# The selection of keys for tokens 128 to 255 moves behind the convolution, and tokens 0 to 127 get no index scores

## The reference, cut to what matters

```
topk = min(TOPK_MAX, seq // 4)                     # 128
limit = (q_pos // CHUNK + 1) * CHUNK               # CHUNK 64
visible = key_pos[None, :] < limit[:, None]
rel = relu(einsum('bqhd,bsd->bqhs', iqb, ik))      # 4 index heads of 64
score = einsum('bqhs,bqh->bqs', rel, iwb)
score = where(visible[None], score, -inf)
_, idx = lax.top_k(score, topk)
valid = idx < limit[None, :, None]
```

## Time and profile before

| | us |
|---|---|
| median of 3 runs | 3282.81 |
| lowest, highest | 3281.57, 3286.73 |
| profiled execution, its own time | 3312.99 |
| its span | 3311.1 |

### The profile page before, as it was taken

How to read it: one execution, slowest core, us unless ns; L and a number is a source line. 1 busy time by engine, 2 the same in 40 slices (tenths; PEclk the granted TensorE clock), 3 DMA queues, 4 the chain that set the end, 5 groups by cost and what they waited for, 6 DMA issues and landing times. The chain is left out here.

```text
span 3311.1 us, 41588 instructions
## 1 busy us (share of the span) xinstructions
PE 2814.8 (85%) x14662; PEld 2084.6 (63%) x14662; DVE 1630.6 (49%) x3068; ACT 993.3 (30%) x1557; POOL 749.0 (23%) x353
## 2 busy tenths in 40 slices
PE   3996777986987787986986889999997988789997
PEld 2784355334775264324884678878886856678886
DVE  6786643335786743236715664643638143441113
ACT  4524422114524422114215631111113231231222
POOL 1430021111430021110320032222323300134443
PEclk9987887998987887997998989999998986699999
DMA  6630017953620027952611021322423210022222
GB/s 235 227 116 33 1 54 303 345 205 123 241 97 31 1 92 295 350 199 80 220 66 58 14 77 58 134 102 77 159 72 113 95 54 1 26 101 92 99 92 73
DMA packets 92342, 398.13 MB, mean 120 GB/s; under 512 B 16384, under 2 KB 18080, under 8 KB 70816
## 3 DMA queue, kind: packets, MB, share of 16 engines
q1 hardware_dynamic: 63248, 303.36, 25.7%
q0 software_dynamic: 28800, 92.30, 7.5%
q10 hardware_dynamic: 144, 0.52, 0.0%
HBM read 489.98 MB, written 23.59 MB: 155 GB/s over the span
## 5 line engine op out<-in xcount | busy, mean ns | idle before, releaser
L2414 DVE TENSOR_TENSOR ffn_silu<-ffn_silu,PS 128x512 f32<-128x512 f32 x66 | 37.6, 597 | 414.6 <-ACT ffn_silu L2396 414.6
L391 POOL TENSOR_TENSOR 19_w_part<-weights_raw,19_w_part 128x2048 fp32r<-128x2048 f32 (+2 forms) x44 | 146.3, 3327 | 406.5 <-ACT 19_w_part L347 406.5
L2147 PE MATMUL PS<-one_weights_more,11_h_tokens 128*64 128x512 f32 (+1 forms) x1024 | 230.9, 603 | 2.6 <-ACT 11_h_tokens L2199 1.7
L233 PE MATMUL PS<-ffn_h_parts,19_w_part 128*128 128x512 f32 (+1 forms) x640 | 203.5, 338 | 8.6 <-DVE ffn_out_t L1687 7.8
L234 PE MATMUL PS<-ffn_h_parts,19_w_part 128*128 128x512 f32 (+1 forms) x640 | 202.4, 338 | 0.0
L391 POOL TENSOR_TENSOR 33_w_part<-weights_raw,33_w_part 128x2048 fp32r<-128x2048 f32 (+2 forms) x36 | 149.4, 4150 | 212.6 <-ACT 33_w_part L347 212.6
L391 POOL TENSOR_TENSOR 3_w_part<-weights_raw,3_w_part 128x1024 fp32r<-128x1024 f32 (+1 forms) x52 | 142.3, 2737 | 237.5 <-ACT 3_w_part L347 237.4
L2147 PEld LDWEIGHTS PS<-one_weights_more,11_h_tokens 128*64 128x64 f32 x1024 | 78.4, 139 | 132.8 <-issue 129.0
L233 PE MATMUL PS<-one_mix_h_parts,3_w_part 128*128 128x512 f32 x352 | 144.3, 410 | 20.2 <-ACT 3_w_part L347 20.2
L2396 ACT ACTIVATE ffn_silu<-PS 128x512 f32<-128x512 f32 x66 | 32.4, 526 | 404.0 <-PE PS L238 378.4
L234 PE MATMUL PS<-one_mix_h_parts,3_w_part 128*128 128x512 f32 x352 | 142.3, 404 | 0.0
(11 more groups left out here) (630 smaller groups left out, 6994.9 us busy)
## 6 DMA issues: line engine op xcount, KB each, us to landing
one_weights_more<-in_w_gu SPq DMA_DIRECT2D x128, 1024.0 KB, 8.7
one_weights_more<-in_w_down SPq DMA_DIRECT2D x64, 1024.0 KB, 8.4
weights_raw<-in_f_gu SPq DMA_DIRECT2D x44, 1024.0 KB, 4.8
one_values<-in_w_ada POOLq DMA_DIRECT2D x32, 1024.0 KB, 6.7
weights_raw<-in_w_proj SPq DMA_DIRECT2D x60, 512.0 KB, 3.4
ffn_shared<-in_w_ada POOLq DMA_DIRECT2D x24, 1024.0 KB, 7.1
weights_raw<-in_w_ada SPq DMA_DIRECT2D x32, 512.0 KB, 9.0
two_ab_mod_w<-in_w_ada POOLq DMA_DIRECT2D x16, 1024.0 KB, 5.4
```

The lines of the kernel that those rows point to most:

```text
L233: nc.tensor.matmul(out, w[0], x[1], start=(j == 0), stop=False)
L391: self.nc.gpsimd.tensor_tensor(self.part[:, u, 1], self.raw[:, u], self.part[:, u, 0].bitcast(F32), ALU.subtract).then_inc(self.count["spl ...
L2147: mm = nc.tensor.matmul(M.PS[rows(h), 2 + i % 2, :], h_[:, i % 2, k, rows(h)], weights(i, h, k * 2 * FE), start=(k == 0), stop=(k == KD - 1))
L2414: ins = nc.vector.tensor_tensor(sl[:, u, off:off + nt], sl[:, u, off:off + nt], M.PS[:, 4 * u + 2 + a, 0:nt], ALU.mult)
```

## The change

- `Values` keeps item 1 only (384 keys, tile 2), so its TensorE queue is: scores 1, chunk 0, chunk 1, chunk 2, chunk 3. Behind the selection VectorE writes tile 0's bias with the two memsets (`choose_all`, with a semaphore of its own).
- Item 3 (the 128-key scores of tile 0) is not computed any more, neither its matmuls nor VectorE's reads and sums.
- Item 2 (256 keys, tile 1) goes to `convolve`. TensorE issues its four matmuls behind the turned row of line 766, VectorE does the selection behind its last convolution. It has one bank, number 7, and a scratch of its own; three semaphores are added.

```diff
--- before.py
+++ after.py
@@ -662,7 +662,7 @@
 def convolve(nc, M, A, l, B):
 
 
-    s = take(M, "par step conv gates sig act_step ab_done tr cp dec_in")
+    s = take(M, "par step conv gates sig act_step ab_done tr cp dec_in scored taken chosen")
     rows = NH_M
     with ExitStack() as ctx:
         cw = ctx.enter_context(M.nc.sbuf_tensor(f"{M.blocks}_conv_w", [P, 4, CONV + 1], F32))
@@ -676,6 +676,9 @@
         a = ctx.enter_context(M.nc.sbuf_tensor(f"{M.blocks}_i_rel", [rows, T], F32))
         am = ctx.enter_context(M.nc.sbuf_tensor(f"{M.blocks}_i_max", [rows, T], F32))
         th = ctx.enter_context(M.nc.sbuf_tensor(f"{M.blocks}_floor", [rows, T], F32))
+
+        keys = SelectKeys(nc, M, {"scored": s["scored"], "taken": s["taken"], "step": s["chosen"]}, B, range(2, 3), (7,),
+                          SelectKeys.scratch(nc, M, ctx))
         block = ctx.enter_context(nc.Block())
 
         @block.sync
@@ -724,6 +727,7 @@
             nc.vector.tensor_scalar(th[:], th[:], -1.0, 80.0, ALU.mult, ALU.min).then_inc(s["ab_done"], 1)
             for c in range(1, 4):
                 conv(c)
+            keys.choose(dve)
 
         @block.scalar
         def _(act):
@@ -766,6 +770,7 @@
                 mm = nc.tensor.transpose(M.PS[:, 6, t * NH_M:(t + 1) * NH_M], a[:, t * P:(t + 1) * P],
                                          M.K[0:rows, K_ID:K_ID + rows])
             mm.then_inc(s["tr"], 1)
+            keys.scores(pe, 2)
     give(nc, s)
 
 
@@ -821,10 +826,6 @@
                     dve.wait_ge(s["taken"], n + 1)
                     step(nc.vector.tensor_tensor(sc[:, 0:w], sc[:, 0:w], tmp[:, 0:w], ALU.add))
 
-            if t == 0:
-                step(nc.vector.memset(B.bias[:, 0, 0:w], 0.0))
-                step(nc.vector.memset(B.bias[0:64, 0, 64:w], NEG))
-                continue
             step(nc.vector.memset(sc[0:64, w - 64:w], -3.0e38))
             src = sc
             for r in range(TOPK // 8):
@@ -833,6 +834,12 @@
                 src = work
             step(nc.vector.tensor_tensor(tmp[:, 0:w], work[:, 0:w], sc[:, 0:w], ALU.is_equal))
             step(nc.vector.tensor_scalar(B.bias[:, t, 0:w], tmp[:, 0:w], NEG, None, ALU.mult))
+
+    def choose_all(self, dve):
+
+        step = Steps(dve, self.s["all"])
+        step(self.nc.vector.memset(self.B.bias[:, 0, 0:P], 0.0))
+        step(self.nc.vector.memset(self.B.bias[0:64, 0, 64:P], NEG))
 
 
 def attend(nc, M, items, scale):
@@ -2616,9 +2623,9 @@
 
     def __init__(self, nc, M, ctx, weights, N, out, tiles, following, before, B=None, scratch=None):
         self.nc, self.M, self.N, self.out, self.tiles, self.before = nc, M, N, out, tiles, before
-        self.s = s = take(M, STREAM + "psum_free copied scored taken step")
+        self.s = s = take(M, STREAM + "psum_free copied scored taken step all")
         self.S = Stream(nc, M, ctx, s, weights, N, following, before.S)
-        self.K = SelectKeys(nc, M, s, B, range(1, TT), (2, 3, 6, 7), scratch) if B else None
+        self.K = SelectKeys(nc, M, s, B, range(1, 2), (2, 3, 6, 7), scratch) if B else None
 
     def free(self, eng, n):
         eng.wait_ge(self.s["psum_free"], n + 3)
@@ -2671,13 +2678,14 @@
         elif self.before.H:
             pe.wait_ge(self.before.s["h_done"], len(self.before.H.order))
         for n in range(N):
-            if K and n + 1 < TT:
+            if K and n + 1 in K.which:
                 K.scores(pe, n + 1)
             S.one(pe, chunk, n, n % 2)
 
     def vector(self, dve):
         if self.K:
             self.K.choose(dve)
+            self.K.choose_all(dve)
 
     def scalar(self, act):
         nc, M, s, S = self.nc, self.M, self.s, self.S
```

## The result

| | median | runs, lowest to highest |
|---|---|---|
| before | 3286.73 us | 5, 3281.57 to 3301.82 |
| changed | 3318.29 us | 5, 3310.22 to 3326.03 |

A forecast was written before the change was run, and what follows sets the result against it. TensorE was taken to bound the projection's block and ScalarE the convolution's end, where VectorE had 6.49 us of slack. -30.8 + 40.5 + 1.0 = +10.7 us on 3282.81 gave 3293.5 us, range 3285 to 3301.

The forecast's parts named there:

- The projection's block: Value projection: TensorE's wait, the scores and the slow restart go; 16.0 us less in layer 0, 14.8 in layer 1.
- take 11.3: Third value chunk's length in us without the wait, bounded by the fourth's 10.88 and the second's 11.62.
- rival 4: Projection's block: another wait holds the third or fourth chunk, a tenth to a third of 30.8 us unsaved; chance 0.05.
- Behind the convolution: End of the convolution block: the moved 256-key scores and selection add 20.2 us per layer, 40.5 together.
- the cycle: Behind the convolution: one head's score matmul, VectorE's read and handovers over the one bank, 1.81 us.
- Rival 2: Behind the convolution: TensorE at 2.4 GHz, only +15.2 us per layer, not slower, 3282.4 us; chance 0.08.
- The rule of the Trainium skill: Convolution's small matmuls: sustained activity releases the throttle, so 10.9 us of back-to-back matmuls should have gone to 2.4 GHz.
- A cost of +1.0: Attention: starting after an 18 us TensorE idle costs 1.0 us in all, ends 0 and +3.
- rival 3: Attention longer at the low clock after the idle, or handovers 0.4 us dearer: +14 to +18 us; chance 0.09.
- The median of the runs shown: Whole kernel before: base time of 3282.81 us to which the +10.7 us was added.
- (its three runs lie over 5.2 us): Whole kernel: ground for taking 0.2%, 6.6 us, as about what a measurement can tell from no change.
- Which I take to lie evenly over the kernel: Whole kernel: the profiled execution's 30.2 us (0.9%) over the runs' median, taken as evenly spread and carried over.

The follow-up runs named there:

- split kernel: Changed kernel with the 256-key scores, reads and ten of 16 rounds back in the projection's block, six rounds behind the convolution: 3277.45 us, 0.9945 of before.
- the profile without the selection: Changed kernel without any selection (scores and rounds) for tokens 128 to 255: 3269.31 us, 0.9910 of before.
- the cut kernel of before: Kernel before, ended behind the first block's two layers and the final norm, the second block's layers left out: mean 1526.7 us of 5 runs.
- the memsets: Kernel before with 22 memsets of a small tile on VectorE behind the last convolution, no selection moved: 3311.90 us, 1.0046 of before.

## Why the prediction was wrong in size and right in sign

**The projection's block, right.** From the first copy to the last, both layers shrank as forecast and by 1.1 us more. Two terms were mis-sized. The third chunk, "take 11.3", came in 10.88, and the second, which the forecast kept at 11.51 from copy to copy in layer 0, came in 10.88 too. The reason given, that VectorE is at work beside them, is refuted: it was busy for 10.21 of 10.80 us beside the second chunk, which yet took 10.88, and in the split kernel for as much beside a chunk of 11.26. The two stretches:

```profile
229.00:239.80 10.80, 10.80 (x98) 10.80 (x97) 10.21 (x26) 2.89 (x2) 4.61 (x1) 1.00 0.04 14
```

```profile
254.10:265.40 11.30, 11.29 (x97) 11.09 (x95) 10.34 (x35) 1.02 (x1) 0.00 (x0) 1.00 0.07 26
```

What makes a chunk of the same matmuls longer or shorter isn't known. The fourth chunk's weights were in time, so rival 4 is refuted.

**Behind the convolution, right.** Scores took 1.22 us as worked out, the cycle 1.79 to 1.88 (1.81), the rounds 15.74 (15.75); the first MAX8 came 10.48 us behind the convolution (10.23). +20.9 and +20.8 against +20.2. Rival 2, a high clock, fell: 0.50 over 10.9 us of four-row matmuls and over the scores. The rule of the Trainium skill that I weighed there (TensorE: Matmul & The Clock Gate, Part 1: sustained matmul activity releases the throttle) would have led to "not slower". The trace disagrees with it here (0.50 with TensorE busy for 10.85 of 10.90 us), and in the gated stage too, where the clock fell from 2.4 to 1.2 GHz with TensorE busy and stayed there for 54.70 of 54.70 busy us. Rival 2's own sum has a slip that changes nothing else: passes that halve from 0.85 to 0.43 make its cycle 1.38 us and not 1.31, and its total 0.4 us more.

**Attention, no cost.** "A cost of +1.0" was -0.7, which is within what profiles of one kernel differ by: the changed kernel's layer 1 took 51.43 us in its first profile and 50.54 in its second. The idle of 18.77 us ahead of attention lengthened nothing that followed (rival 3 fell).

**The base, wrong.** "The median of the runs shown" was three runs at the low end: 93 runs of before have a mean of 3299.3 and a standard deviation of 8.8 us, so the median of three was 16.5 too low. "(its three runs lie over 5.2 us)" was read as how finely this kernel can be measured; with 8.8 us, a mean of three runs is good to about 5 (8.8 over the root of 3). That alone hardly makes 16.5; what else set those three low isn't known. This is the largest part of the miss.

**"Which I take to lie evenly over the kernel", wrong.** The 30.2 us by which before's profiled execution exceeded the shown median were a sign of uneven time. The late gated stage of that execution ran 54.7 us at the low clock; its length was 66.90 us there and 46.20 in the profile without the selection (2750.68 to 2796.88), a difference of 20.7 in one stage. Had I looked for the stretches with a busy TensorE at 0.50, I would have found it, and would have asked in which of its lengths the changed kernel falls. No rival of mine was of this kind. It is worth some 8 us here, with a standard error near 3: +20.4 in whole kernels, +11.5 to +12.7 without the stage.

The account: 3293.5 + 16.5 for the base + about 8 of the late stage + 1 or 2 of a local cost of 11.5 to 12.7 where I had 10.7 = about 3320, measured 3318.3 and in all 15 runs 3319.7. The base and the local cost are shown. That the 8 us come from the stage rests on leaving it out, within that error; why the stage costs the changed kernel more is not shown.

## What to carry to other kernels

Before work is moved into a block's slack, write down how long the slack is and move only that much: six of sixteen rounds fit and won 18 us, sixteen with their handovers over one PSUM bank lost 20 (12 of them without the late stage). When the profiled execution is longer than the runs by more than they differ among themselves, find the stage that holds the excess, or take the base as uncertain by that amount. Judge a local edit in a cut kernel as well: no stage far behind it can blur it, and its runs spread less (12.9 us for the cut kernel of before, 20.3 for five runs of the whole one). Take the length of a delay from its own rows before its cost is held against a sum: the memsets lasted 14.1 us and not 11.7.

## What was not expected of the hardware

- TensorE's granted clock fell to 1.2 GHz and stayed there for 54.70 us with the engine busy for 54.70 of them, in the gated stage; there it was high for 6.8, 13.7 or 30.7 us first, with the same instructions.
- That length went with where the clock had risen behind the stage's first matmul: after 2.9 to 4.0 us, 4.4 us, or 5.9 to 6.2 us for 30.7, 6.8 and 13.7 us, in eleven profiles.
- A shift of that stage's start by some 2 us moved the mean of whole kernels by +10.8 us in one kernel and by -8.5 in another.
- Value chunks of the same matmuls took 10.88 us in one kernel and 11.26 in another, at the high clock (1.00) and with VectorE selecting beside both.
